# First attention: the causal mask moved from TensorE to VectorE in phases 1 to 7, and filling tiles moved

## The chip, the cores and the metric

One core of a Trainium2 chip runs the whole kernel. The metric is the device time of one execution in microseconds (us). The kernel before took 2174.97 us (median of three runs, 2171.95 to 2177.67).

## What is computed

Two transformer blocks over 512 tokens of width 1024. The change lies in the attention of the first block, which has 8 query heads of width 64 in two groups of four. Its selected branch and its window branch both reduce here to causal softmax attention over all 512 keys, because 16 selected blocks of 64 keys would be more than the 8 there are and the window is as long as the sequence:

```
def masked_softmax(logits, mask):
    logits = jnp.where(mask, logits, NEG)
    return jnp.where(mask, jax.nn.softmax(logits, axis=-1), 0.0)

# per query block of 128
pc  = masked_softmax(qb @ kc.T, cmp_end <= t)      # compressed keys, 31 of them
o_c = pc @ vc
ps  = masked_softmax(qb @ ks.T, kpos <= t);  o_s = ps @ vs
pw  = masked_softmax(qb @ kw.T, kpos <= t);  o_w = pw @ vw
o   = gates[0] * o_c + gates[1] * o_s + gates[2] * o_w
```

## The kernel before

Every matrix product is made of three fp32r matmuls (high by high, high by low, low by high). TensorE carries the whole kernel; ScalarE makes the high parts, VectorE and GpSimd the low ones.

The heads are taken in four pairs, one head of each group, both at once. A pair has two branches, so there are eight *phases* of four query blocks, 32 *steps* numbered here (phase, block). Even phases are the first branch, odd ones the second. `scores(j, i)` calls `head_scores` (L702 to L714): it waits until the exponentials of the step before have read PSUM banks 2 and 3 (`A["exps"]`), runs six matmuls (two heads in two halves of the array, three parts) over 128 to 512 keys, and then for each head one matmul of the identity with a 128x128 triangle of 0 and -1e30 (`causal_r`), which adds the mask to the diagonal block; the last one signals `A["scores"]`. VectorE's `head_peaks` (L1336 to L1339) waits for that and takes the negated row maximum of both heads; ScalarE's `head_exps` makes the two exponentials with their sums (L2003), `A["exps"]`; VectorE normalises (L1343, L1347). One phase later TensorE turns the probabilities (`turn`, L723), ScalarE copies the high part, VectorE's `head_low` subtracts for the low part (L1149, `A["lo"]`), and `values` multiplies (L731).

Once a pair, behind the last step of an odd phase, `cmp_scores` computes the logits of the next pair over the compressed keys into the same banks (L750 the mask, L756 24 matmuls of 32 columns). It waits for the exponentials; the next phase's first scores wait for VectorE's subtraction `s_cs["sub"]` (L1380). `cmp_turn` and `cmp_values`, which use a pair's compressed probabilities, stand in the first step of the even phase behind the pair (phases 2, 4, 6 and 8).

The waits of TensorE are covered by *filling tiles*: `fill(n)` runs n times three matmuls over 512 columns (L517 to L519) of the projections that are needed next (q of the next pair, the merge gates), 152 tiles in all. The order is written out by hand in `NSA_FILL`: one tuple a phase, one entry a step. The first number runs after the scores, the second at the step's end, the third (in steps (2,0), (4,0), (6,0), (8,0)) between `cmp_turn` and `cmp_values`. VectorE and ScalarE count the same numbers (`nsa_made`) to know which unit to evict after which step. VectorE's queue also carries the 31-tap convolution of the other branch of the block, two taps a step (L1209).

Each engine works its queue in order, and the queues meet only at semaphores.

Of the kernel before, what the change touches and what calls it, by code (L numbers as in the profile page):

```python
# [17 lines left out]
P = 128  # L18
# [148 lines left out]
EARLY_TAPS = 62  # L167
EARLY_IDLE = 8
LN_ADD = ((0, 1), (4, 0), (7, 3))
NSA_FILL = [((2, 2),) * 4] + [((2, 2),) * 4, ((2, 2, 2), (2, 1), (2, 2), (2, 1))] * 4  # L170


def nsa_made(j, i):
# [35 lines left out]
def build(nc, x_in, p_in, weights, vectors, last_gain, out):  # L209
# [4 lines left out]
    with ExitStack() as ctx:  # L214
# [145 lines left out]
        def stage_sems(stage, *names):  # L360
            return {n: sem(f"{stage}_{n}") for n in names}
# [6 lines left out]
        s_ln = stage_sems("ln", "sum", "mean", "cent", "sq", "acc", "var", "sd", "inv", "bc", "n", "act", "hi", "lo")  # L368
        s_mix = stage_sems("mix", "a", "b", "hi", "lo")
        att_names = ("scores", "peak", "exps", "inv", "probs", "turned", "hi", "lo", "pv", "ohi", "olo")  # L370
        A1 = stage_sems("nsa", *att_names, "q", "qhi")
        s_cs = stage_sems("cmp_att", "scores", "sub", "exp", "stat", "probs")
        A2 = stage_sems("fox", *att_names, "qk", "qkhi", "vturned", "vhi", "vlo", "crow")
        s_fg = stage_sems("forget", "dve", "act")
# [139 lines left out]
        def _(pe):  # L514
# [186 lines left out]

            def head_scores(A, s, qi, terms):  # L702

                if s:
                    pe.wait_ge(A["exps"], 2 * s)
                n = (qi + 1) * P
                qs = slice(qi * P, n)
                for t, (a, b) in enumerate(terms):
                    for hd in range(2):
                        rows = slice(hd * HD, (hd + 1) * HD)  # L710
                        pe.matmul(ps[:, 2 + hd, 0:n], a[rows, qs], b[rows, 0:n], start=t == 0, stop=False)  # L711
                for hd in range(2):
                    mm = pe.matmul(ps[:, 2 + hd, qs], ident_r[:], causal_r[:], start=False, stop=True)  # L713
                mm.then_inc(A["scores"], 1)  # L714

            def head_turn(A, y, kb, probs):
# [21 lines left out]
            def fill(n):  # L738

                for at in range(made[0], made[0] + n):  # L740
                    part(u0 + at // DC, at % DC, at % DC + 1)
                made[0] += n
# [55 lines left out]
            for j in range(9):  # L798
                b = j - 1
                for i in range(QB):  # L800
                    pieces = NSA_FILL[j][i]
                    if j < 8:
                        if j == 0 and i == 0:
                            cmp_scores(0)
                            fill(pieces[0])
                        scores(j, i)
                    if j or i:
                        fill(pieces[0])
                    else:
                        gates_turn()  # L810
                    if j == 8 and i == 0:
                        pe.wait_ge(s_ln["sum"], 3)
                        pe.wait_ge(A1["exps"], 64)
                        pe.matmul(ps[:, 2, :], mean_ch[:], ln_sum[:], start=True, stop=True).then_inc(s_ln["mean"], 1)
                    if b >= 0:
                        if i:
                            values(b, i - 1)
                        elif b:
                            values(b - 1, QB - 1)
                            if b % 2:  # L820
                                cmp_turn(b // 2)
                                fill(pieces[2])
                                cmp_values(b // 2)
                        turn(b, i)
                    if j % 2 and i == QB - 1 and j < 7:
                        cmp_scores(j // 2 + 1)
                    fill(pieces[1])
            fill(4)
            values(7, QB - 1)
# [309 lines left out]
        def _(dve):  # L1139
# [195 lines left out]

            def head_peaks(A, s, qi, st):  # L1336

                dve.wait_ge(A["scores"], s + 1)
                dve.tensor_reduce(st[:, 0, :, qi:qi + 1], ps[:, 2:4, 0:(qi + 1) * P], AX.X, ALU.max, negate=True).then_inc(A["peak"], 1)  # L1339

            def head_normalise(A, s, qi, st, probs, gate=None):
# [1161 lines left out]
```

## Time and profile before

| | us |
|---|---|
| median of three runs | 2174.97 |
| the profiled execution | 2177.95 |
| its span, first to last instruction | 2176.2 |
| TensorE busy | 2145.6 |
| VectorE, ScalarE, GpSimd busy | 1005.7, 873.2, 933.2 |

Busy times overlap, and matmuls are pipelined, so TensorE's busy time is no measure of its peak. The first attention lies between about 123 and 345 us of the span. Mean granted clock of TensorE: 0.995 of full speed.

### The profile page before, as it was taken

How to read it: one execution, taken by the hardware profiler on the slowest of the kernel's cores; microseconds unless marked ns; L12 is line 12 of the kernel's file. 1: busy time of each engine (PE TensorE's matmuls, PEld its weight loads, DVE VectorE, ACT ScalarE, POOL GpSimd, SP SyncE). 2: the span in 40 equal slices, each digit the busy share in tenths (PEclk: the TensorE clock that was granted, in tenths of full speed). 3: DMA queues.
4: the chain of work that ended last, by engine and by line, in shares of the span. 5: the costliest groups of instructions: out<-in, count | busy, mean ns of one | idle time of the engine just before them, and what ended most of it. 6: DMA issues, size and time to landing. Idle time of an engine off the chain costs nothing.

```text
span 2176.2 us, 25317 instructions
## 1 busy us (share of the span) xinstructions
PE 2145.6 (99%) x10198; PEld 1758.0 (81%) x10198; DVE 1005.7 (46%) x1630; ACT 873.2 (40%) x1366; POOL 933.2 (43%) x424
## 2 busy tenths in 40 slices
PE   9999999999999999999999999999999999999998
PEld 7877778888888887777778888888888888888886
DVE  5887775355525235566535422314643354222134
ACT  5444345344424254555434422324532244233234
POOL 5731224444444455322235444444554454444446
PEclk9999999999999999999999999999999999999999
DMA  4421113233333232211122223332223323233322
GB/s 160 151 82 40 49 40 95 89 107 97 97 97 97 97 112 83 68 49 59 49 68 88 97 97 97 97 97 84 91 90 98 95 86 97 97 97 97 97 82 84
DMA packets 53829, 193.27 MB, mean 89 GB/s; under 512 B 6096, under 2 KB 6224, under 8 KB 53712
## 3 DMA queue, kind: packets, MB, share of 16 engines
q1 hardware_dynamic: 52992, 189.81, 27.6%
q10 hardware_dynamic: 720, 1.84, 0.3%
q8 instruction: 81, 1.33, 0.2%
q14 instruction: 36, 0.29, 0.0%
HBM read 189.53 MB, written 2.10 MB: 88 GB/s over the span
## 4 chain that ended last, share of the span: by engine, by line
PE 91%; DVE 4%; ACT 3%; issue 1%; DMA 0%; POOL 0%; DVEq 0%; ACTq 0%; POOLq 0%
PE ps L517 27%; PE ps L519 27%; PE ps L518 27%; PE ps L731 1%; PE ps L980 1%; PE ps L711 1%; ACT w_hi L1854 1%; PE ps L723 1%; PE ps L998 1%; PE ps L613 1%; ACT fprob L1993 1%; PE ps L1005 1%; DVE xg_lo L1169 1%; PE ps L713 0%; PE ps L1007 0%
## 5 line engine op out<-in xcount | busy, mean ns | idle before, releaser
L470 POOL TENSOR_TENSOR w_lo<-w_raw,w_hi 128x1024 fp32r<-128x1024 f32 x352 | 851.8, 2421 | 1203.8 <-ACT w_hi L1854 1203.7
L517 PE MATMUL ps<-xg_hi,w_hi 128*128 128x512 f32 x1688 | 672.6, 398 | 4.5 <-POOL w_lo L484 2.4
L519 PE MATMUL ps<-xg_hi,w_lo 128*128 128x512 f32 x1688 | 660.0, 391 | 0.0
L518 PE MATMUL ps<-xg_lo,w_hi 128*128 128x512 f32 x1688 | 659.5, 391 | 0.0
L1854 ACT ACTIVATE w_hi<-w_raw 128x1024 fp32r<-128x1024 f32 x352 | 372.2, 1057 | 626.8 <-PE ps L519 623.9
L517 PEld LDWEIGHTS ps<-xg_hi,w_hi 128*128 128x128 f32 x1688 | 318.2, 189 | 68.1 <-issue 2.6
L519 PEld LDWEIGHTS ps<-xg_hi,w_lo 128*128 128x128 f32 x1688 | 317.9, 188 | 67.4
L518 PEld LDWEIGHTS ps<-xg_lo,w_hi 128*128 128x128 f32 x1688 | 318.5, 189 | 59.7
L517 PE MATMUL ps<-h_hi,w_hi 128*128 128x512 f32 x688 | 267.6, 389 | 0.0
L518 PE MATMUL ps<-h_lo,w_hi 128*128 128x512 f32 x688 | 267.6, 389 | 0.0
L519 PE MATMUL ps<-h_hi,w_lo 128*128 128x512 f32 x688 | 267.6, 389 | 0.0
L1143 DVE TENSOR_TENSOR ps<-ps,inv_rms 128x512 f32<-128x512 f32 x164 | 113.6, 695 | 194.2 <-PE ps L519 181.1
L517 PEld LDWEIGHTS ps<-h_hi,w_hi 128*128 128x128 f32 x688 | 129.1, 188 | 27.0
L519 PEld LDWEIGHTS ps<-h_hi,w_lo 128*128 128x128 f32 x688 | 129.1, 188 | 26.7
L518 PEld LDWEIGHTS ps<-h_lo,w_hi 128*128 128x128 f32 x688 | 129.1, 188 | 26.7
L1499 DVE TENSOR_TENSOR mixed<-mixed,ps 128x512 f32<-128x512 f32 x48 | 33.0, 687 | 200.0 <-PE ps L519 200.0
L1169 DVE SCALAR_TENSOR_TENSOR xg_lo<-resid,vec,xg_hi 128x512 fp32r<-128x512 f32 x72 | 87.2, 1215 | 12.5 <-ACT xg_hi L1880 10.3
L1209 DVE SCALAR_TENSOR_TENSOR ps<-glu,vec,ps 128x512 f32<-128x512 f32 x116 | 87.1, 751 | 1.8
L1843 ACT ACTIVATE h_hi<-ps 128x512 fp32r<-128x512 f32 x86 | 51.5, 599 | 89.7 <-DVE ps L1760 48.8
L1880 ACT ACTIVATE xg_hi<-resid,vec 128x512 fp32r<-128x512 f32 x72 | 51.7, 718 | 63.4 <-DVE resid L1499 40.2
L479 POOL TENSOR_TENSOR sq_sum<-sq_sum,sq 128x512 f32<-128x512 f32 x42 | 66.4, 1581 | 24.6 <-ACT sq L1877 22.3
L1760 DVE TENSOR_TENSOR ps<-tile_b,ps 128x512 f32<-128x512 f32 x64 | 44.5, 696 | 57.7 <-ACT tile_b L2301 57.7
(344 smaller groups left out, 2459.3 us busy)
## 6 DMA issues: line engine op xcount, KB each, us to landing
w_raw<-in_weights SPq DMA_DIRECT2D x352, 512.0 KB, 3.5
out_x<-mixed SPq DMA_DIRECT2D x8, 256.0 KB, 2.1
resid<-in_x SPq DMA_DIRECT2D x3, 512.0 KB, 7.2
p_raw<-in_p ACTq DMA_DIRECT2D x3, 512.0 KB, 3.7
resid<-in_x SPq DMA_DIRECT2D x2, 256.0 KB, 3.6
last_gain<-in_last_gain SPq DMA_DIRECT2D x1, 512.0 KB, 4.5
w_raw<-in_weights SPq DMA_DIRECT2D x1, 256.0 KB, 3.7
w_raw<-in_weights ACTq DMA_DIRECT2D x1, 256.0 KB, 4.0
```

The lines of the kernel that those rows point to most:

```text
L470: pool.tensor_tensor(w_lo[:, slot, :], w_raw[:, u % RAW, :], w_hi[:, slot, :].bitcast(F32), ALU.subtract).then_inc(w_ready, 1)
L479: pool.tensor_tensor(sq_sum[:], sq_sum[:], sq[:, m % 2:m % 2 + 1, :], ALU.add).then_inc(summed, 1)
L517: pe.matmul(o, w, x, start=start, stop=False)
L518: pe.matmul(o, w, xl, start=False, stop=False)
L519: return pe.matmul(o, wl, x, start=False, stop=stop)
L1143: dve.tensor_tensor(out, ps[:, BANK[u]:BANK[u] + 1, :], R[:], ALU.mult).then_inc(done, 1)
L1169: dve.scalar_tensor_tensor(xg_lo[:, m:m + 1, :], X[:, m:m + 1, :], g, xg_hi[:, m:m + 1, :].bitcast(F32), ALU.mult, ALU.subtract).then_inc( ...
L1209: ins = dve.scalar_tensor_tensor(acc if k < CONV_TAPS - 1 else conv_acc[:, ct, :], src, w, acc, ALU.mult, ALU.add)
L1760: dve.tensor_tensor(t, T2[:, m % 2:m % 2 + 1, :], t, ALU.mult).then_inc(s_mlp["s"], 1)
L1843: act.activation(out, x, ACT.Copy, scale=scale).then_inc(done, 1)
L1854: act.activation(w_hi[:, u % RING, :], w_raw[:, u % RAW, :], ACT.Copy).then_inc(w_hi_ready, 1)
L1880: act.activation(xg_hi[:, m:m + 1, :], X[:, m:m + 1, :], ACT.Copy, scale=g).then_inc(prep_hi, 1)
```

## The change

From step (1,0) on, TensorE leaves the two mask matmuls out, and the last of the six score matmuls signals. VectorE adds the triangle to the diagonal block of both heads in PSUM, in place, in one instruction of 128x256, and waits for its own add before it takes the maximum. In phase 0 the mask stays where it was.

`NSA_FILL` changes in phases 1 to 8. Odd phases: step 2 has one tile fewer at its end; step 3 has two tiles between the last turn and `cmp_scores` and one behind it, where there were two behind (in phase 7, without compressed scores, the same numbers). Even phases: step 0 has one tile fewer at its end, step 3 one more. So one tile more stands ahead of the scores of steps (3,0), (5,0), (7,0), the fifth of their pair's eight. The sums per phase stay 16.

```diff
-NSA_FILL = [((2, 2),) * 4] + [((2, 2),) * 4, ((2, 2, 2), (2, 1), (2, 2), (2, 1))] * 4
+NSA_FILL = [((2, 2),) * 4] + [((2, 2), (2, 2), (2, 1), (2, 1, 2)), ((2, 1, 2), (2, 1), (2, 2), (2, 2))] * 4
...
-        A1 = stage_sems("nsa", *att_names, "q", "qhi")
+        A1 = stage_sems("nsa", *att_names, "masked", "q", "qhi")
...
-                        pe.matmul(ps[:, 2 + hd, 0:n], a[rows, qs], b[rows, 0:n], start=t == 0, stop=False)
-                for hd in range(2):
-                    mm = pe.matmul(ps[:, 2 + hd, qs], ident_r[:], causal_r[:], start=False, stop=True)
+                        mm = pe.matmul(ps[:, 2 + hd, 0:n], a[rows, qs], b[rows, 0:n], start=t == 0,
+                                       stop=s >= QB and t == len(terms) - 1)
+                if s < QB:
+                    for hd in range(2):
+                        mm = pe.matmul(ps[:, 2 + hd, qs], ident_r[:], causal_r[:], start=False, stop=True)
                 mm.then_inc(A["scores"], 1)
...
                     if j % 2 and i == QB - 1 and j < 7:
+                        fill(pieces[2])
                         cmp_scores(j // 2 + 1)
+                    elif j == 7 and i == QB - 1:
+                        fill(pieces[2])
                     fill(pieces[1])
...
+                diagonal = ps[:, 2:4, qi * P:(qi + 1) * P]
                 dve.wait_ge(A["scores"], s + 1)
+                if s >= QB:
+                    dve.tensor_tensor(diagonal, diagonal, causal_r[:].bitcast(F32).unsqueeze(1).to_broadcast([P, 2, P]),
+                                      ALU.add).then_inc(A["masked"], 1)
+                    dve.wait_ge(A["masked"], s - QB + 1)
                 dve.tensor_reduce(st[:, 0, :, qi:qi + 1], ps[:, 2:4, 0:(qi + 1) * P], AX.X, ALU.max, negate=True).then_inc(A["peak"], 1)
```

## Rows read from the trace of the kernel before

**Rows 1.** The page: busy time by engine; the chain that ended last.
```profile
PE 2145.6 (99%) x10198; PEld 1758.0 (81%) x10198; DVE 1005.7 (46%) x1630; ACT 873.2 (40%) x1366; POOL 933.2 (43%) x424
...
PE 91%; DVE 4%; ACT 3%; issue 1%; DMA 0%; POOL 0%; DVEq 0%; ACTq 0%; POOLq 0%
```

**Rows 2.** Groups by line, 120 to 345 us: count, busy us, mean ns, idle before.
```profile
L713 PE MATMUL ps<-causal_r,ident_r 128*128 128x128 f32 x64 | 14.4, 307 | 0.0
```

**Rows 3.** Busy time by stretch, PE PEld DVE ACT POOL; then clock, DMA share, GB/s.
```profile
189.70:213.70 24.00, 23.48 (x151) 18.68 (x150) 20.49 (x38) 10.28 (x26) 4.79 (x2) 1.00 0.16 53
```

**Rows 4.** Timeline of TensorE in step (3,0): start us, us, engine, line.
```profile
189.69 0.33 PE L711 MATMUL ps<-kk_hi,q_hi 64*128 64x128 f32 x2
...
190.17 0.44 PE L713 MATMUL ps<-causal_r,ident_r 128*128 128x128 f32 x2
190.44 0.45 PE L517 MATMUL ps<-xg_hi,w_hi 128*128 128x512 f32 x1
190.73 0.40 PE L518 MATMUL ps<-xg_lo,w_hi 128*128 128x512 f32 x1
```

**Rows 5.** Timeline of TensorE behind the compressed scores of (3,3).
```profile
212.12 0.50 PE L517 MATMUL ps<-xg_hi,w_hi 128*128 128x512 f32 x1
212.45 0.39 PE L518 MATMUL ps<-xg_lo,w_hi 128*128 128x512 f32 x1
```

**Rows 6.** Groups of VectorE by line and shape, 120 to 345 us.
```profile
L1149 DVE TENSOR_TENSOR pt_lo<-ps,pt_hi 128x256 fp32r<-128x256 f32 x8 | 3.4, 419 | 2.0 <-ACT pt_hi L1843 2.0
...
L1143 DVE TENSOR_TENSOR ps<-ps,inv_rms 128x512 f32<-128x512 f32 x3 | 2.1, 688 | 0.0
```

**Rows 7.** Timeline of VectorE, steps (2,1) to (2,3); in brackets its idle time.
```profile
176.46 0.69 DVE L1339 TENSOR_REDUCE stat<-ps 128x2 f32<-128x512 f32 x1
...
185.43 0.69 DVE L1149 TENSOR_TENSOR pt_lo<-ps,pt_hi 128x512 fp32r<-128x512 f32 x1 [0.36 <-ACT pt_hi L1843]
...
186.73 1.23 DVE L1339 TENSOR_REDUCE stat<-ps 128x2 f32<-128x1024 f32 x1
...
189.47 0.17 DVE L1343 RECIPROCAL stat<-stat 128x2 f32<-128x2 f32 x1 [0.85 <-ACT prob_s L2003]
189.67 1.00 DVE L1347 TENSOR_SCALAR prob_s<-prob_s,stat,gates 128x512 f32<-128x512 f32 x2
```

**Rows 8.** Timeline of TensorE: first scores of step (2,1).
```profile
174.90 0.39 PE L711 MATMUL ps<-kk_hi,q_hi 64*128 64x256 f32 x2
```

**Rows 9.** Timeline: phase 2's first turned tile, subtraction and values.
```profile
195.71 1.23 DVE L1149 TENSOR_TENSOR pt_lo<-ps,pt_hi 128x1024 fp32r<-128x1024 f32 x1 [0.23 <-ACT pt_hi L1843]
...
197.15 0.40 PE L731 MATMUL ps<-pt_hi,vv_hi 128*128 128x512 f32 x1
```

**Rows 10.** Timeline, TensorE and VectorE, scores (3,1) to scores (4,0).
```profile
194.88 0.38 PE L711 MATMUL ps<-kk_hi,q_hi 64*128 64x256 f32 x2
...
197.50 0.69 DVE L1339 TENSOR_REDUCE stat<-ps 128x2 f32<-128x512 f32 x1
...
207.48 1.23 DVE L1339 TENSOR_REDUCE stat<-ps 128x2 f32<-128x1024 f32 x1 [0.56 <-PE ps L713]
...
210.33 0.41 PE L750 MATMUL ps<-cmp_mask_r,ident_r 128*128 128x128 f32 x2 [0.52 <-ACT prob_w L2003]
...
212.84 0.42 DVE L1380 TENSOR_TENSOR prob_c<-ps,c_stat 128x248 f32<-128x248 f32 x1
...
213.71 0.33 PE L711 MATMUL ps<-kk_hi,q_hi 64*128 64x128 f32 x2
```

**Rows 11.** Waits of TensorE, 120 to 345 us: total, times, longest.
```profile
PE ps L750 <- ACT prob_w L2003: 1.6, 3, 0.5
```

**Rows 12.** Busy time by stretch, columns as in rows 3.
```profile
163.90:167.30 3.40, 3.40 (x13) 2.26 (x12) 0.84 (x3) 0.41 (x1) 0.00 (x0) 0.51 0.02 5
...
259.70:266.50 6.80, 6.80 (x25) 5.16 (x24) 2.83 (x8) 2.16 (x6) 0.99 (x1) 0.51 0.00 0
```

**Rows 13.** Waits of VectorE, 120 to 345 us.
```profile
DVE pt_lo L1149 <- ACT pt_hi L1843: 28.7, 25, 3.1
```

## Prediction

> **What bounds the kernel now.** I read the page first: TensorE is busy 99% of the span and carries 91% of the chain that ended last [rows 1]. So a matmul taken away is worth its slot, unless another engine is late at that place. The change touches only the first attention, about 127 to 307 us. Its stage has two more things to see. In the list of groups, the causal-mask matmuls are 64 [rows 2], two a step. In the table by stretch, phase 3 (189.7 to 213.7) keeps VectorE busy 20.49 of 24.0 us [rows 3], convolution taps included, and what is left is mostly waiting inside its own loop (for exponentials, for turned probabilities). So VectorE is close to being the second bound here. I call a step (phase, query block), both from 0; mask changes are in phases 1 to 7, 28 steps.
>
> The loop of a step: scores (TensorE) -> maximum (VectorE) -> two exponentials (ScalarE) -> next scores, since banks 2 and 3 are used once at a time. Tiles that fill stand between.
>
> **Part 1, TensorE loses 56 mask matmuls.** Before: mask pair 190.17, first filling matmul 190.44, second 190.73 [rows 4]. With a mask the second filling matmul starts 0.29 after the first; where no mask stands between (after the compressed scores), 212.12 to 212.45, 0.33 [rows 5]. So a step saves 190.44 - 190.17 = 0.27 to 0.28 less 0.04 for the switch of the array that moves to the filling matmul: 0.24. 28 x 0.24 = **-6.7 us**. The signal of the scores also comes some 0.3 earlier, worth something only where VectorE is idle.
>
> The Trainium skill speaks against this size: "TensorE: Matmul & The Clock Gate", section "Back-to-back issue gap", gives about 81 ns for each 128-column matmul in a stream with its weight load. By it the pair costs 0.16 us and the change would bring, as an estimate, 28 x 0.16 = 4.5 us, 2.2 us less than my term. The rows show 0.27 for the pair, so the trace doesn't agree, and I keep it.
>
> **Part 2, VectorE gets 28 adds of 128x256 in PSUM, each with a wait for itself.** The trace has no such add. Nearest: the subtraction 128x256 out of PSUM, 0.419; the 128x512 product PSUM to PSUM, 0.688 [rows 6]. The maximum may start only when the add has landed: a reciprocal of 0.17 started at 189.47 and its successor, which waits for it, at 189.67, so 0.03 to 0.04 on top [rows 7]. I take 0.46, by the subtraction, which has the same width; ends 0.34 (half of the 512-wide product, no wait) and 0.72 (all of it, with the wait). In all 28 x 0.46 = 12.9 us of VectorE. Whether it costs depends on where VectorE leads the chain. Three places:
>
> *The fifth step of a pair, (2,3) to (3,0), three times.* From the maximum of (2,1) at 176.46 to that of (2,3) at 186.73 VectorE has only 0.36 us of waiting [rows 7], so it works 10.27. After: two more adds, 10.27 + 0.92 - 0.3 = 10.9. The maximum of (2,1) came 1.56 after its scores (174.90 [rows 8]); now + 0.46 for its own add and + 0.69 because one filling tile fewer stands at the end of (2,0) and the scores come that much nearer to VectorE's long subtraction: 2.71. From the maximum of (2,3) to the end of its exponentials, which released the reciprocal at 189.47, are 2.74 [rows 7]. Sum 16.35. TensorE walks from scores (2,1) to scores (3,0) in 189.69 - 174.90 = 14.79 [rows 4, 8], less 3 x 0.24, plus 0.69 for the tile moved ahead: 14.76. So it waits some 1.5 us where it waited next to nothing: 3 x 1.5 = **+4.5** (ends 0.5, if VectorE drops more waiting than I see, and 1.9). The moved tile pays for only 0.69 of it.
>
> *Values after the second scores of an odd phase, four times.* The subtraction of phase 2's first turned tile runs 195.71 to 196.94 and the matmuls that read it start at 197.15 [rows 9]: slack 0.21. Its chain goes back through ScalarE's queue (exponentials of (3,0), w_hi, q_hi, o_hi, then the turned tile) to the maximum of (3,0), which comes 0.46 later, while TensorE arrives two masks (0.48) earlier: 0.46 + 0.48 - 0.21 = 0.73. Not every phase has q_hi and o_hi in that queue, so I take 0.6: 4 x 0.6 = **+2.4** (ends 0 and 4.1).
>
> *Compressed scores, three times.* Now TensorE waits 0.52 for the exponentials of (3,3) [rows 10]; 1.6 us in all three [rows 11]. TensorE's way from scores (3,1) 194.88 to 210.33 is 15.45, 14.8 without the wait; after, less 0.72 for masks, plus 0.69 (one tile fewer at the end of (3,2), two before the compressed scores), plus the 0.6 just found: 15.4. VectorE: maximum (3,1) 2.62 after its scores, now about 3.6; from it to the maximum of (3,3) 207.48 - 197.50 = 9.98, less 0.56 of waiting that goes, plus 0.92: 10.34; 2.74 to the end: 16.7. Wait 1.2 or so instead of 0.65: the moved filling thus doesn't remove this wait. Behind them only one filling tile stands (two before) ahead of scores (4,0), which need VectorE's subtraction; it ended 213.26 and the scores came at 213.71 [rows 10], slack 0.45, now 0.45 - 0.69: a new wait of 0.24, or 0.45 when VectorE comes late to them. Together 0.55 + 0.35 = +0.9 each (ends 0 and 1.9): **+2.7**.
>
> *Moves themselves.* 152 filling tiles before and after, no DMA or copy added. Each new block of filling after a turn costs one start, 0.1: +0.3. The weights keep up: GpSimd, which makes their low parts, is busy 4.79 of 24.0 us [rows 3].
>
> Sum: -6.7 + 4.5 + 2.4 + 2.7 + 0.3 = **+3.2 us**.
>
> **The clock.** In two stretches right behind compressed scores the granted clock is 0.51, TensorE at 1.2 GHz: 3.4 us at 163.9 and 6.8 us at 259.7; behind the ones at 210.33, the last of phase 3, it stayed at 1.00, 2.4 GHz [rows 3, 12]. Both falls come just after TensorE had waited some 0.5 us [rows 11] and then run the narrow matmuls of the compressed scores. Cost 0.49 x 3.4 + 0.49 x 6.8 = 5.0 us in this execution. It took 2177.95 (span 2176.2 and 1.75 around); the median of the runs, 2174.97, is 2.98 lower, so a typical run seems to lose some 2 us here. The idle ahead of these places gets longer, not shorter; the full-width tile that is now put directly before them speaks for fewer falls. I take half a fall more, 0.5 x 2.5 = +1.2.
>
> From the execution's own time: 2177.95 + 3.2 + 1.2 - 2.98 = 2179.4 (the same from the median: 2174.97 + 4.4).
>
> **Rivals.**
> A, faster: VectorE hides the adds in its waits (28.7 us before subtractions of turned tiles alone [rows 13]), the compressed scores find their exponentials ready and the clock holds. Then 2174.97 - 6.7 - 2.0 - 2.1 + 0.3 = 2164.5. For it: that sum is twice 12.9. Against it: most of them lie just behind the compressed scores, where slack was several us anyway; the tight stretches have 0.36. Chance 0.12.
> B, slower: the longer idle before the compressed scores makes the clock fall every time. It decides once TensorE idles there for longer than now (0.65 with the switch) in all three. Three falls of 2.5 are 7.5 against 2 typical: 2174.97 + 3.2 + 5.5 = 2183.7; one more fall at the new waits of the fifth step, 2186. Against: the wait at 210.33 was as long as the others and the clock held [rows 3, 10]. Chance 0.30.
> C, break-even: the three waits come at half (9.6 to 4.8), since one wait absorbs the next one's lag: 2174.97 - 6.7 + 4.8 + 0.3 = 2173.4. Chance 0.20.
> My forecast, +3 to +6.5: 0.38 (its own range 2178 to 2182).
>
> **Numbers.** What can be told from no change is 0.3%, 6.5 us: faster is below 2168.4, slower above 2181.5. Slower: most of B (0.25) and the upper quarter of the forecast (0.10): 0.35. Faster: most of A: 0.10. Same 0.55. The range leaves out half of A and the end of B: 2167 to 2187. The fifth step and the compressed scores take 2 adds each, the values one: 16 adds on the chain, so an add of 0.34 takes 1.9 us off and one of 0.72 puts 4.2 on.
>
> **What would show it.** Right: the profile after shows VectorE adds near 0.43; mask matmuls 8; scores (3,0), (5,0), (7,0) preceded by TensorE idle of over 1 us ended by ScalarE's exponentials; new waits of the values matmuls on VectorE's subtraction; the wait before compressed scores above 0.5. Wrong: waits of TensorE in 142 to 307 under 3 us in all (then A), or a clock below 1.00 for over 15 us of the stage (then B). If the pair of mask matmuls was really 0.16, the pitch from last scores to second filling matmul shrinks less than 0.24.

## The result

| | device us, median | lowest to highest | runs |
|---|---|---|---|
| before | 2174.40 | 2171.95 to 2177.67 | 6 |
| after | 2186.64 | 2185.51 to 2190.18 | 6 |

The ratio is 1.0059 with a 95% interval of 1.0049 to 1.0069: 12.2 us slower, clear of what such a measurement can tell. The forecast was 2179.4; the result lies at the upper end of its range, beside rival B's second figure (2186). The profiled execution took 2186.16 us, span 2184.4.

Later runs of the kernel before bring it to 95 (median 2174.77). Two executions that were slow throughout (one of before, 3825.87 us; one of mixed_tap, 2368.89) are left out. Each run comes with its mean granted clock, so its span (the time less 1.75 us) can be split: span x (1 - mean clock) is lost to TensorE's slower level, and the rest of the span is work and waits. I use this split throughout. It takes half of every moment at the lower level as lost work; one run's clock is read to 0.001, 2.2 us, so only means say something (with their standard errors). The loss is that of the whole span: in every profile some 3 us of it lie in the last 15 us, and single falls come elsewhere too, with or without the change. Only differences between kernels speak of the change.

| kernel | runs | mean us | lost to the clock | the rest |
|---|---|---|---|---|
| before | 95 | 2174.5 | 5.9 +- 0.3 | 2166.9 +- 0.2 |
| after | 6 | 2187.1 | 12.4 +- 0.5 | 2172.9 +- 0.7 |

Of +12.6 us in the means, 6.0 are work and waits and 6.5 are the clock.

**The profile after.** The page: busy time by engine, and the chain that ended last. TensorE's share of the chain fell from 91% [rows 1] to 86%; VectorE's and ScalarE's doubled or nearly so.
```profile
PE 2143.4 (98%) x10142; PEld 1753.2 (80%) x10142; DVE 1017.6 (47%) x1658; ACT 872.4 (40%) x1366; POOL 933.2 (43%) x424
...
PE 86%; DVE 8%; ACT 5%; issue 1%; DMA 0%; POOL 0%; DVEq 0%; ACTq 0%; POOLq 0%
```
Groups by line in the stage (count, busy us, mean ns, idle before): 8 mask matmuls are left of 64 [rows 2], and the addition costs what its neighbour of the same width costs [rows 6], 426 ns.
```profile
L716 PE MATMUL ps<-causal_r,ident_r 128*128 128x128 f32 x8 | 1.8, 301 | 0.0
...
L1348 DVE TENSOR_TENSOR ps<-ps,causal_r 128x256 f32<-128x256 f32 x28 | 11.9, 426 | 2.6 <-PE ps L712 2.6
```
Waits of TensorE in 120 to 345 us (total, times, longest), to be held against rows 11. L712 are scores, L753 compressed scores, L734 values, L817 the mean of the LayerNorm. They sum to 12.6 us, 9.8 of them not the LayerNorm's; before had 1.6 at the compressed scores and 0.9 elsewhere (a wait of 0.2 ahead of the first compressed scores, which every kernel has, is left out).
```profile
PE ps L712 <- ACT prob_s L2015: 3.9, 6, 1.0
PE ps L753 <- ACT prob_w L2015: 3.0, 3, 1.3
PE ps L817 <- DVE ln_sum L1427: 2.8, 1, 2.8
PE ps L734 <- DVE pt_lo L1155: 2.3, 5, 0.9
PE ps L712 <- DVE prob_c L1392: 0.6, 3, 0.2
```
TensorE's timeline at the places of rows 4, 9, 10: scores (3,0), values of phase 2's first tile, compressed scores, scores (4,0); in brackets how long it had idled. The first wait began at about 190.87 and is the forecast's fifth step; 0.86 is the values' wait; 0.89 answers to 0.52 [rows 10].
```profile
191.90 0.33 PE L712 MATMUL ps<-kk_hi,q_hi 64*128 64x128 f32 x2 [1.03 <-ACT prob_s L2015]
...
192.71 0.39 PE L518 MATMUL ps<-xg_lo,w_hi 128*128 128x512 f32 x1
...
199.95 0.47 PE L734 MATMUL ps<-pt_hi,vv_hi 128*128 128x512 f32 x1 [0.86 <-DVE pt_lo L1155]
...
213.80 0.41 PE L753 MATMUL ps<-cmp_mask_r,ident_r 128*128 128x128 f32 x2 [0.89 <-ACT prob_w L2015]
...
216.77 0.33 PE L712 MATMUL ps<-kk_hi,q_hi 64*128 64x128 f32 x2 [0.23 <-DVE prob_c L1392]
```
From these scores to the second filling matmul are 192.71 - 191.90 = 0.81, before 190.73 - 189.69 = 1.04 [rows 4]: the mask's slot was 0.23.

VectorE's timeline ahead of that first wait (rows 7 are the same stretch before). The subtraction, one convolution tap (L1215), the addition, the maximum (L1351), then ScalarE's exponentials, which release the reciprocal at 191.88 and TensorE's scores at 191.90. The addition is late by the tap and by everything ahead of it.
```profile
187.41 0.69 DVE L1155 TENSOR_TENSOR pt_lo<-ps,pt_hi 128x512 fp32r<-128x512 f32 x1 [0.36 <-ACT pt_hi L1855]
188.02 0.75 DVE L1215 SCALAR_TENSOR_TENSOR ps<-glu,vec,ps 128x512 f32<-128x512 f32 x1
188.67 0.43 DVE L1348 TENSOR_TENSOR ps<-ps,causal_r 128x256 f32<-128x256 f32 x1
189.13 1.23 DVE L1351 TENSOR_REDUCE stat<-ps 128x2 f32<-128x1024 f32 x1
...
191.88 0.17 DVE L1355 RECIPROCAL stat<-stat 128x2 f32<-128x2 f32 x1 [0.85 <-ACT prob_s L2015]
```
Something I hadn't foreseen, at the end of the stage: VectorE's last LayerNorm addition started 0.19 us behind a subtraction on GpSimd and took 2.70 us, and TensorE waited for it.
```profile
313.38 2.34 POOL L470 TENSOR_TENSOR w_lo<-w_raw,w_hi 128x1024 fp32r<-128x1024 f32 x1 [3.78 <-ACT w_hi L1866]
...
313.57 2.70 DVE L1427 TENSOR_TENSOR ln_sum<-ln_sum,conv_acc 128x512 f32<-128x512 f32 x1
...
316.32 1.51 PE L817 MATMUL ps<-ln_sum,mean_ch 128*128 128x512 f32 x2 [2.84 <-DVE ln_sum L1427]
```
Table by stretch (columns of rows 3), behind the first and the third compressed scores and behind that last wait. At 0.76 to 0.85 a part of the stretch is at the 1.2 GHz level (each of these three falls cost 1.7 us in all, the first running on past its stretch); behind the second compressed scores it held 2.4 GHz throughout.
```profile
163.81:168.00 4.19, 4.01 (x36) 3.33 (x37) 3.12 (x8) 0.54 (x2) 0.00 (x0) 0.85 0.07 24
...
213.80:218.00 4.20, 3.97 (x38) 3.24 (x39) 3.44 (x9) 0.54 (x2) 0.00 (x0) 1.00 0.06 22
...
262.81:270.00 7.19, 7.02 (x49) 5.80 (x50) 5.58 (x14) 2.29 (x7) 0.57 (x1) 0.76 0.01 2
...
316.30:324.00 7.70, 7.68 (x33) 5.70 (x34) 1.25 (x2) 1.12 (x2) 0.00 (x0) 0.78 0.19 68
```
The two profiled executions happen to lose the same in the stage, 5.1 us each by a table in steps of 2.5 us, so between these two the clock explains nothing. The 6.5 us show only in the means over all runs.

### The profile page after: what moved, and what is told of

It reads as the page before. It is cut to its first block, busy times and chain, and to the rows that moved or that the text cites. A ratio compares the mean times of both kernels' runs of the same rounds, so it can differ in the third digit from the quotient of the medians.

```text
span 2184.4 us, 25233 instructions
## 1 busy us (share of the span) xinstructions
PE 2143.4 (98%) x10142; PEld 1753.2 (80%) x10142; DVE 1017.6 (47%) x1658; ACT 872.4 (40%) x1366; POOL 933.2 (43%) x424
## 4 chain that ended last, share of the span: by engine, by line
PE 86%; DVE 8%; ACT 5%; issue 1%; DMA 0%; POOL 0%; DVEq 0%; ACTq 0%; POOLq 0%
PE ps L517 27%; PE ps L519 26%; PE ps L518 26%; DVE stat L1351 1%; ACT w_hi L1866 1%; PE ps L986 1%; DVE ps L1215 1%; DVE pt_lo L1155 1%; PE ps L1004 1%; PE ps L613 1%; ACT prob_w L2015 1%; ACT fprob L2005 1%; PE ps L1011 1%; ACT pt_hi L1855 1%; DVE xg_lo L1175 0%
## 5 line engine op out<-in xcount | busy, mean ns | idle before, releaser
L1175 DVE SCALAR_TENSOR_TENSOR xg_lo<-resid,vec,xg_hi 128x512 fp32r<-128x512 f32 x72 | 86.4, 1204 | 12.2 <-ACT xg_hi L1892 10.0
L1215 DVE SCALAR_TENSOR_TENSOR ps<-glu,vec,ps 128x512 f32<-128x512 f32 x116 | 87.1, 751 | 1.9
L1164 DVE TENSOR_TENSOR sq_sum<-sq_sum,ps 128x512 f32<-128x512 f32 x57 | 39.1, 687 | 69.4 <-ACT ps L1883 69.0
```

What stands on the lines that cost most here:

```text
L1164: dve.tensor_tensor(sq_sum[:], sq_sum[:], ps[:, NB:NB + 1, :], ALU.add).then_inc(summed, 2 if m == DC - 2 and in_two_parts(n) else 1)
L1175: dve.scalar_tensor_tensor(xg_lo[:, m:m + 1, :], X[:, m:m + 1, :], g, xg_hi[:, m:m + 1, :].bitcast(F32), ALU.mult, ALU.subtract).then_inc( ...
L1215: ins = dve.scalar_tensor_tensor(acc if k < CONV_TAPS - 1 else conv_acc[:, ct, :], src, w, acc, ALU.mult, ALU.add)
```

## The experiments

Sixteen kernels. Theory 1: VectorE's additions make it late at a few places, TensorE idles there, and its clock falls behind the idling. A ratio is taken against executions of the kernel before that ran beside the kernel in question.

| kernel | us, median | ratio, 95% interval | lost to the clock | the rest |
|---|---|---|---|---|
| adds_old_fill | 2185.22 | 1.0049 [1.0037, 1.0062] | 10.0 +- 1.5 | 2173.6 +- 1.5 |
| fill_only | 2171.93 | 0.9990 [0.9981, 0.9999] | 6.3 +- 0.7 | 2164.6 +- 0.3 |
| masks_gone | 2168.92 | 0.9976 [0.9965, 0.9986] | 5.9 +- 0.9 | 2161.5 +- 0.7 |
| ln_early | 2185.34 | 1.0046 [1.0033, 1.0058] | 11.8 +- 1.5 | 2171.0 +- 0.8 |
| both | 2188.08 | 1.0057 [1.0045, 1.0069] | 11.4 +- 1.1 | 2174.0 +- 0.5 |
| ln_late | 2175.12 | 1.0003 [0.9994, 1.0011] | 6.7 +- 0.9 | 2166.9 +- 0.5 |
| ln_later | 2179.70 | 1.0026 [1.0016, 1.0036] | 9.0 +- 1.0 | 2168.9 +- 0.6 |
| taps_spread | 2184.52 | 1.0045 [1.0033, 1.0057] | 10.5 +- 1.3 | 2171.4 +- 0.6 |
| taps_spread_pe | 2178.45 | 1.0016 [1.0007, 1.0025] | 6.1 +- 0.3 | 2170.7 +- 0.3 |
| stuffed | 2182.39 | 1.0043 [1.0030, 1.0056] | 7.9 +- 1.5 | 2173.6 +- 0.9 |
| tap_behind | 2178.62 | 1.0024 [1.0014, 1.0034] | 10.3 +- 0.7 | 2167.0 +- 0.6 |
| adds_last | 2174.26 | 1.0000 [0.9991, 1.0009] | 8.3 +- 0.9 | 2165.0 +- 0.6 |
| mixed | 2177.36 | 1.0011 [1.0003, 1.0020] | 7.3 +- 0.5 | 2167.8 +- 0.3 |
| mixed_tap | 2173.34 | 0.9992 [0.9983, 1.0001] | 7.5 +- 0.7 | 2164.0 +- 0.2 |
| stuffed_values | 2177.88 | 1.0016 [1.0007, 1.0025] | 9.1 +- 0.9 | 2167.4 +- 0.5 |
| tap_behind_pe | 2171.48 | 0.9991 [0.9982, 0.9999] | 7.1 +- 0.7 | 2163.8 +- 0.5 |

### Which part costs: four kernels

**adds_old_fill**: the mask moved, the filling as before.
```diff
-NSA_FILL = [((2, 2),) * 4] + [((2, 2), (2, 2), (2, 1), (2, 1, 2)), ((2, 1, 2), (2, 1), (2, 2), (2, 2))] * 4
+NSA_FILL = [((2, 2),) * 4] + [((2, 2),) * 4, ((2, 2, 2), (2, 1), (2, 2), (2, 1))] * 4
```


> The adds and the missing mask matmuls of the change, with the filling order of before. Theory 1 (VectorE's queue is late, and the adds lie on the chain at the fifth step, at the values and at the compressed scores): waits of TensorE for exponentials before compressed scores above 1.5 us each, 1.2 to 1.8 us before scores (3,0), (5,0), (7,0); time 2183 to 2190, as slow as the change. Rival (the moved filling tiles make the loss, since one tile fewer stands before scores (2k,0) and at the end of (2k,0)): near 2172.

**fill_only**: the new filling, the masks on TensorE, no additions (the first line of the change's diff and the three fill(pieces[2]) lines alone).

> The new filling order alone, masks on TensorE. Theory 1: the waits before the compressed scores (0.5 us each) go, others stay, 2171 to 2176; clock falls behind the compressed scores fewer than before. Rival (the moved tiles make the loss): 2180 or more.

**masks_gone**: neither masks on TensorE nor additions, from phase 1 on.
```diff
-                if s >= QB:
-                    dve.tensor_tensor(diagonal, diagonal, causal_r...
-                    dve.wait_ge(A["masked"], s - QB + 1)
```


> The change without VectorE's adds: the causal mask of phases 1 to 7 is left out altogether, so the output differs. Theory 1: 28 x 0.24 us less of TensorE and no new waits beyond 0.5 us: 2166 to 2170. If the mask pairs were worth only 0.16 us each, 2170 to 2173. Rival (the time is lost by the shorter score groups or by the clock, not by the adds): 2178 or more.

**ln_early**: the last LayerNorm addition a step earlier.
```diff
-LN_ADD = ((0, 1), (4, 0), (7, 3))
+LN_ADD = ((0, 1), (4, 0), (7, 2))
```


> The change, with the last addition of the LayerNorm sum one step earlier in VectorE's queue (after step (7,2) instead of (7,3)). In the changed kernel that addition took 2.70 us (0.68 before) while GpSimd's subtraction ran, TensorE waited 2.84 us for it and its clock fell to 0.50 behind. Theory 2 (this is the loss that the forecast lacks, 5 us): wait of the mean matmul for ln_sum gone, no fall at 317 us, 2180 to 2183. Rival (the wait is that of the lagging exponentials of (7,3), and would only be named otherwise): 2185 to 2188.

The additions are the loss, whatever the filling: masks_gone, without them, is as fast as expected. With the old filling TensorE's waits at the six places are longest (1.14 to 1.72 us, one of the three at the compressed scores below the 1.5 expected), and in this profile the clock falls behind each of the six: the table by stretch of adds_old_fill behind its compressed scores (first, third and fifth line) and behind the first scores of phases 3, 5 and 7 (second, fourth and sixth).
```profile
163.50:169.50 6.00, 6.00 (x38) 4.63 (x37) 3.45 (x9) 0.95 (x4) 0.00 (x0) 0.72 0.01 3
190.00:197.00 7.00, 5.83 (x30) 5.11 (x31) 5.22 (x14) 4.21 (x13) 0.98 (x1) 0.76 0.19 69
214.50:220.50 6.00, 6.00 (x32) 4.62 (x32) 4.15 (x11) 2.16 (x6) 0.00 (x0) 0.72 0.02 4
241.00:248.00 7.00, 5.82 (x30) 5.15 (x31) 5.70 (x14) 4.19 (x12) 0.98 (x1) 0.76 0.17 67
265.00:272.00 7.00, 7.00 (x49) 5.59 (x48) 4.79 (x12) 1.88 (x6) 0.00 (x0) 0.76 0.01 2
291.00:300.00 9.00, 7.55 (x39) 6.04 (x39) 7.33 (x16) 4.98 (x12) 2.04 (x1) 0.81 0.16 58
```
Its waits (as above), then those of fill_only, where the ones of rows 11 are gone:
```profile
PE ps L712 <- ACT prob_s L2012: 5.3, 5, 1.7
PE ps L753 <- ACT prob_w L2012: 4.3, 3, 1.6
```
```profile
PE ps L711 <- ACT prob_s L2006: 0.7, 2, 0.4
PE ps L731 <- DVE pt_lo L1152: 0.3, 1, 0.3
```
But idling isn't needed for a fall. fill_only came in at its expected time, yet its clock loss, 6.3, is no lower than before's 5.9, though fewer falls were expected. Its table by stretch, where TensorE's compressed scores ran from 211.00 to 212.7 with no idle ahead of them:
```profile
210.00:212.50 2.50, 2.50 (x30) 2.21 (x30) 2.22 (x5) 0.47 (x3) 0.00 (x0) 1.00 0.41 162
...
215.00:217.50 2.50, 2.50 (x8) 1.92 (x7) 2.24 (x6) 1.75 (x5) 0.33 (x1) 0.50 0.00 0
```
masks_gone has such a fall behind its first compressed scores. So some falls come with the narrow matmuls of the compressed scores or what stands around them, and what the additions bring are falls more.

In the column "the rest" the change falls into three steps: the filling brings 2166.9 to 2164.6 (-2.3), taking the masks off 2164.6 to 2161.5 (-3.1), the additions 2161.5 to 2172.9 (+11.4), and their clock +6.5 (5.9 to 12.4). ln_early took the 2.8 us wait away and brought 1.9 of "the rest" (standard error of the difference 1.1); its addition took 1.12 us. The clock loss stayed, and at 2185.34 it missed the 2180 to 2183 expected: the LayerNorm is not the main part of the miss.

### The additions alone, and TensorE's idling filled

**both**: the kernel before, masks and filling as they were, plus the 28 additions (the first attention's VectorE lines of the diff alone).

> The kernel before, with its causal-mask matmuls and its filling kept, plus VectorE's 28 additions: the mask is added twice, which leaves the probabilities of masked keys at zero. It prices the additions alone. Theory 1 (the additions stretch the chain scores, maximum, exponentials; TensorE waits at the three places and its clock falls there more often): TensorE's waits as in the run with additions and the old filling (about 1.2 to 1.7 us at every compressed scores and at every first step of an even phase), the clock loss of the stage again near 10 us instead of 5, and the masks' 6.7 us on TensorE paid in part only, since at the steps with a wait they fill it: 2188 to 2193. Rival (the removal of the masks is itself what makes the clock fall, since TensorE is less busy): clock loss as before (5 us), 2183 or less.

2188.08, the highest of all. "The rest" rose by 7.1 and the clock loss by 5.5. The rival, that only a TensorE without masks has its clock fall, is out: here it has all of them. Beside adds_old_fill: 56 mask matmuls taken off, under the additions, bring 2.9 us in the median and 0.4 +- 1.6 in "the rest", since TensorE waits anyway.

**stuffed**: 24 matmuls more, where the changed kernel idled.
```diff
+            def again():
+                ...
+                three(o, wh, xh, wl, xl, k == 0, False)
+                pe.matmul(o, wh, xh, start=False, stop=k == 0)
...
                         fill(pieces[2])
+                        again()
                         cmp_scores(j // 2 + 1)
...
                     fill(pieces[1])
+                    if i == QB - 1 and j in (2, 4, 6):
+                        again()
```


> The changed kernel with 24 matmuls of 512 columns more on TensorE (four of them, 0.92 us, ahead of the compressed scores of phases 1, 3 and 5 and ahead of the first scores of phases 3, 5 and 7); they add one filling product again, so the output changes. They stand where TensorE waited 0.83 to 1.26 us in the changed kernel, so that it works instead of waiting. Theory 1 (TensorE's clock falls behind those waits): 5.5 us of work are added and 5.0 us or more of waits go, the sum of both stays within 1 us, and the clock falls of the stage become fewer: from a loss of 12 us (mean over the runs) to 7 or less, so that the kernel with more work is faster, 2179 to 2183. Rival (the falls have nothing to do with these waits): the same loss, 2186 to 2189; second rival (the work isn't hidden): 2190 or more.

Its waits: those ahead of scores fell from 3.9 to 0.9, of compressed scores from 3.0 to 0.3; the other two stayed.
```profile
PE ps L827 <- DVE ln_sum L1440: 2.8, 1, 2.8
PE ps L734 <- DVE pt_lo L1168: 2.2, 5, 0.9
PE ps L712 <- ACT prob_s L2028: 0.9, 3, 0.4
...
PE ps L763 <- ACT prob_w L2028: 0.3, 1, 0.3
```
By stretch behind three of the six places (ahead of the third it still idled 0.32) and behind the LayerNorm's wait, which both kernels keep; behind the other three the clock was 1.00 as in the first two lines:
```profile
163.00:168.00 5.00, 4.83 (x44) 3.95 (x45) 4.28 (x10) 1.11 (x6) 0.00 (x0) 1.00 0.04 15
189.00:195.00 6.00, 5.91 (x41) 4.62 (x39) 4.85 (x12) 3.21 (x11) 0.78 (x1) 1.00 0.16 60
...
260.00:268.00 8.00, 7.55 (x52) 6.34 (x53) 5.68 (x14) 2.58 (x10) 1.46 (x1) 0.79 0.04 13
...
313.80:321.50 7.70, 7.69 (x33) 5.80 (x34) 1.24 (x2) 1.16 (x2) 0.00 (x0) 0.78 0.22 68
```
The kernel with 5.5 us more work is 4.3 us faster, in the predicted interval: "the rest" is up by 0.7 and the clock loss down by 4.5 (standard error 1.6), to 7.9 where 7 or less was expected. This is the experiment that shows the clock following the idling.

All eighteen kernels say the same less sharply. A straight line through their mean clock losses against TensorE's waits in the stage by their profiles is 5.9 + 0.48 x waits (all in us; standard error of the slope 0.08, correlation 0.85), with kernels up to 1.9 off it. So about half a microsecond of clock goes with each microsecond of waits, and the changed kernel's 10.1 us more of waits would give 4.9 of its 6.5. The waits are those of one profile each. By the profiles, nearly all falls of the stage lie behind compressed scores, with or without idling there; only adds_old_fill (three, behind the first scores of phases 3, 5 and 7) and taps_spread (one, behind a wait of 1.9) have others, the one behind a long LayerNorm wait apart.

### The LayerNorm addition beside GpSimd

**ln_late** and **ln_later**: the kernel before with one, then two copies ahead of that addition.
```diff
+                    if (j, i) == LN_ADD[2]:
+                        for n in (0, 1):
+                            dve.tensor_copy(T[:, n, :], ps[:, NB, :])
                     if (j, i) in LN_ADD:
```


> The kernel before with one more VectorE copy of 512 columns (about 0.6 us) ahead of the third LayerNorm addition, so that the addition starts beside GpSimd's subtraction, as in the changed kernel, and nothing else of the change. Theory (the addition is stretched by GpSimd's work, not by anything of the masks): the addition goes from 0.68 to 2.3 to 2.8 us, TensorE waits 2.3 to 3 us ahead of the mean, and its clock falls behind that wait: 2176.5 to 2179. Rival (an effect of the changed kernel's memory or queues): the addition stays at 0.7 us, TensorE waits below 0.8 us, and the time stays within 1 us of before.

> The kernel before with two more VectorE copies of 512 columns ahead of the third LayerNorm addition. With one of them the addition still began 0.09 us ahead of GpSimd's subtraction and took 0.68 us; with two it begins about 0.5 us behind its start, as in the changed kernel (0.19 us behind). Theory (an addition of three SBUF tiles on VectorE that starts beside GpSimd's subtraction is held until that ends): 2.0 to 2.8 us, TensorE waits 2.5 to 3 us ahead of the mean, 2177 to 2180. Rival (the 2.70 us came from something else in the changed kernel): 0.68 us, TensorE waits 1.1 us, 2175 to 2176.

With one copy the expected did not happen, because the addition was still ahead of GpSimd by 0.09 us: it took 0.68, and GpSimd's subtraction, 2.34 elsewhere, took 2.82 (ln_late's timeline):
```profile
305.14 0.68 DVE L1415 TENSOR_TENSOR ln_sum<-ln_sum,conv_acc 128x512 f32<-128x512 f32 x1
...
305.23 2.82 POOL L470 TENSOR_TENSOR w_lo<-w_raw,w_hi 128x1024 fp32r<-128x1024 f32 x1 [4.85 <-ACT w_hi L1856]
```
With two it came behind (ln_later's):
```profile
308.47 2.34 POOL L470 TENSOR_TENSOR w_lo<-w_raw,w_hi 128x1024 fp32r<-128x1024 f32 x1 [4.84 <-ACT w_hi L1857]
...
308.98 2.38 DVE L1415 TENSOR_TENSOR ln_sum<-ln_sum,conv_acc 128x512 f32<-128x512 f32 x1
```
GpSimd ends at 308.47 + 2.34 = 310.81, the addition at 311.36, 0.55 later. In the changed kernel it is 315.72 and 316.27, again 0.55. So the second to start does its work when the first is through. TensorE waited 2.76 us and the kernel took 4.9 us more than before, in the expected interval: 2.0 in "the rest", 3.1 (standard error 1.0) at the clock. ln_late, with one copy less and the addition ahead, took 0.4 us more than before. The difference, some 4.6 us, is nearly all the price of the order of two instructions.

### Where in a step: VectorE's taps

**taps_spread** and **taps_spread_pe**: the taps dealt out by a table, with the mask on VectorE and on TensorE.
```diff
+EVEN_TAPS = ((1, 4), (0, 0), (1, 0), (2, 0))
+TAPS = [((2, 0), (2, 0), (1, 0), (3, 0))] + [((2, 0),) * 4, EVEN_TAPS] * 3 + [((2, 0), (2, 0), (2, 0), (0, 0))]
...
-                    if tapped[0] < CT * CONV_TAPS:
-                        taps(1)
+                    if j < 8:
+                        taps(TAPS[j][i][0])
```


> The changed kernel with the 62 convolution taps of VectorE's queue dealt out otherwise in phases 0 to 7 (two a step in odd phases; in even phases five in the first step, four of them behind the low parts of the compressed probabilities, then none, one and two), and the third LayerNorm addition at (7,2). Each tap is about 0.7 us of VectorE, so this takes up to 1.4 us off VectorE's queue at the steps where TensorE waited, and puts it where VectorE had idle time. Theory 1 (the loss is VectorE's lateness at three places, and the clock falls that follow): the waits at the compressed scores, at the first steps of even phases and at the values fall below 0.3 us each, the clock loss of the stage goes from 12 us to below 6, and the 6.7 us of mask matmuls come out as a gain: 2163 to 2169. Rival (the clock falls come from TensorE's thinner stream of instructions without the masks, not from the waits): clock loss stays near 10 us, 2173 to 2180.

> The same deal of taps and the new filling with the causal mask left on TensorE (no additions on VectorE): the control for the run above. It shows what of that run's gain comes from the taps and what from moving the mask. Theory 1: before this deal TensorE's waits were 1 us at most with this filling, so there is little to win: 2168 to 2173, 3 to 7 us above the run with the mask on VectorE. Rival (the deal of taps is the gain): within 1.5 us of that run, or faster.

Both missed. The waits I aimed at shrank (ahead of scores 3.9 to 0.6, of compressed scores 3.0 to 1.7) but did not all fall below 0.3, and others came, for turned tiles. Waits of taps_spread:
```profile
PE ps L736 <- DVE pt_lo L1157: 9.3, 9, 1.9
```
The main reason, read from VectorE's trace and not tested by a run of its own, is that of the LayerNorm addition again. With two taps ahead of it, the normalisation (L1361) of the first and third step of every odd phase runs into GpSimd's subtraction and ends only behind it. Such a pair of instructions takes 0.60 us at 128 columns and 0.87 at 384 elsewhere; here, all four times, 2.43 to 2.45 and 2.94 to 2.95. First the mean of the eight at 128 columns (344 ns in fill_only), then one pair with GpSimd's instruction:
```profile
L1361 DVE TENSOR_SCALAR prob_w<-prob_w,stat,gates 128x128 f32<-128x128 f32 x8 | 9.8, 1259 | 0.1
```
```profile
196.33 2.40 POOL L472 TENSOR_TENSOR w_lo<-w_raw,w_hi 128x1024 fp32r<-128x1024 f32 x1 [6.39 <-ACT w_hi L1867]
196.63 2.45 DVE L1361 TENSOR_SCALAR prob_w<-prob_w,stat,gates 128x128 f32<-128x128 f32 x2
```
Over the eight steps that is 15.6 us more of VectorE. The control has the same eight, also 15.6 us, and is 6.5 us slower than fill_only without any addition. No other kernel here has one such step. So these two runs say little on dealing the taps: they show a collision that the deal brought about.

**tap_behind**: one tap moved, and only at the fourth query block, plus ln_early's edit.
```diff
                     if tapped[0] < CT * CONV_TAPS:
-                        taps(1)
+                        taps(2 if i == 3 and j < 7 else 1)
...
-                    if tapped[0] < CT * CONV_TAPS:
+                    if tapped[0] < CT * CONV_TAPS and not (i == 2 and j < 7):
                         taps(1)
```


> The changed kernel with the third LayerNorm addition at (7,2) (its own run: 2185.3) and, in phases 0 to 6, the convolution tap (0.75 us) that stood ahead of VectorE's addition at the fourth query block moved behind it and the maximum, where VectorE waits for ScalarE's exponentials. Theory 1 (what costs is the lateness of that addition at the six places): the addition starts up to 0.65 us earlier, the waits ahead of the compressed scores fall from 0.8 to 1.3 us to 0.2 to 0.6 us, those of the first scores of odd phases from 1.0 to 0.4 us, and the clock loss falls by 2 to 5 us: 2176 to 2181. Rival (the loss is spread over all 28 additions and TensorE's thinner stream): 2184 to 2186. A tap behind may also make the normalisation late where the exponentials are quick; then the turns wait, and the time stays.

**tap_behind_pe**: the same on fill_only.

> The new filling with the masks on TensorE (2171.9), the tap moved as in the run with the moved tap, and the third LayerNorm addition at (7,2). Here TensorE waits 0.5 us at most, so theory 1 expects nothing of the tap's move: 2171 to 2173, and the value of moving the mask is the difference to 2178.6, a loss of 6 to 7 us. Rival (the tap ahead of the maximum costs in every version): 2167 to 2170.

Both times are as expected. Seven taps moved by one place brought 6.7 us with the additions (against ln_early) and 0.5 without (against fill_only, which lacks ln_early's edit too). In the means it is 5.5: 4.0 +- 1.0 in "the rest", and 1.5 +- 1.6 at the clock, which shows no change there; 2 to 5 was expected. VectorE's timeline (compare the one above): the addition follows the subtraction at once, two taps run while ScalarE makes the exponentials, and TensorE's wait is 0.34 instead of 1.03.
```profile
184.28 0.69 DVE L1155 TENSOR_TENSOR pt_lo<-ps,pt_hi 128x512 fp32r<-128x512 f32 x1 [0.36 <-ACT pt_hi L1855]
184.89 0.42 DVE L1348 TENSOR_TENSOR ps<-ps,causal_r 128x256 f32<-128x256 f32 x1
185.34 1.23 DVE L1351 TENSOR_REDUCE stat<-ps 128x2 f32<-128x1024 f32 x1
186.49 1.54 DVE L1215 SCALAR_TENSOR_TENSOR ps<-glu,vec,ps 128x512 f32<-128x512 f32 x2
188.08 0.17 DVE L1355 RECIPROCAL stat<-stat 128x2 f32<-128x2 f32 x1
```

### Seven of the 28

**adds_last**: fill_only plus the additions of the fourth query block. **mixed**: ln_early without those seven. **mixed_tap**: tap_behind without them.
```diff
-                if s < QB:
+                if s < QB or qi == QB - 1:
                     for hd in range(2):
...
-                if s >= QB:
+                if s >= QB and qi < QB - 1:
                     dve.tensor_tensor(diagonal, diagonal, ...
```


> The kernel before with the new filling (2171.9) and the masks on TensorE, plus VectorE's addition at the fourth query block of phases 1 to 7 alone (7 of the 28; at these the mask is added twice). All 28 additions with the masks kept cost 13 us. Theory 1 (the additions cost where TensorE has no work behind the scores, that is at the end of each phase): these seven carry most of it, 2178 to 2182, with waits of 0.8 us or more at the compressed scores or first scores, and a clock loss of 9 us or more. Rival (each addition costs alike): 7/28 of 13 us, 2174 to 2176, clock loss 6 to 7.5 us.

> The changed kernel with the third LayerNorm addition at (7,2) (2185.3) and the causal mask of the fourth query block of every phase back on TensorE: 21 steps on VectorE instead of 28. Theory 1 (lateness at the end of each phase is what costs): 7 x 0.23 = 1.6 us of mask matmuls come back, the waits at the compressed scores and first scores fall from about 1.0 us by the addition's 0.46 and the mask's 0.23 to about 0.3 us, clock loss from 12 to 7 to 9: 2175 to 2179. Rival (each addition costs alike, 13/28 = 0.46 us each): 2185.3 - 7 x 0.46 + 1.6 = 2183.7.

> The same with the convolution tap moved behind the maximum of the fourth query block (2178.6 with all 28 additions). Theory 1: the tap's 0.65 us covers what was late there, so the waits at the six places are gone, and 21 x 0.23 = 4.8 us of TensorE's work is saved; what stays are the waits at the values of odd phases (0.86 us once, 0.36 us three times): 2169 to 2174, the first version with the mask on VectorE that is not slower than before. Rival (the clock loss of 10 us comes from TensorE's thinner stream, which this keeps in 21 of 28 steps): 2176 to 2179.

The same seven additions cost 2.3 us where they are the only ones (adds_last, the rival's size), and 8.0 us where the other 21 stand too (ln_early against mixed, 1.6 us of mask slots that came back not counted). adds_last thus missed what theory 1 expected, and mixed met it (2177.36, clock loss 7.3). So the places are right, but no addition has a price of its own: where these seven stand alone they go into VectorE's spare time, and behind the other 21 they come out in TensorE's. The two pairs differ in one thing more, which no run separates: adds_last keeps all the masks on TensorE, and their slots give VectorE time. mixed_tap, as expected, is the only kernel with the mask mostly on VectorE that is not slower than before; nor is it faster than fill_only.

**stuffed_values**: tap_behind with two matmuls more ahead of the values of each odd phase's second step.
```diff
                         if i:
+                            if i == 1 and j % 2:
+                                again()
                             values(b, i - 1)
```


> The kernel with the moved tap (2178.6) and two matmuls of 512 columns more (0.46 us) ahead of the values of the second step of phases 1, 3, 5 and 7, where TensorE waited 0.55, 0.86, 0.38 and 0.36 us; the output changes by the added products. Theory 1 (the clock falls behind these waits too): the work is hidden but for 0.2 us, the waits go, the clock loss falls from 10 us to 7 or less: 2175 to 2177. Rival (these waits are too short to matter): clock loss stays at 10, 2178.5 to 2180.

Inconclusive. The waits at values fell from 3.2 to 1.4 us and the time by 0.7; the clock loss of 9.1 +- 0.9 lies between the two expectations.

## Why the prediction was wrong

By its own steps, in means over runs:

- **The clock, forecast +1.2, measured +6.5.** This is the step that failed. I took "half a fall more" by splitting the difference between two arguments, though I had forecast 9.6 us of new waits in the same text and had two falls in front of me, each behind an idle of 0.5 us. The number of falls was not worked out from the waits. Their price wasn't too low: 2.5 was taken, and each fall in the profile after and in adds_old_fill cost 1.7, so 6.5 us are some four of these more, not half a one (both has longer ones, of 3.4 and 5.2). The argument that a full-width tile directly ahead of the compressed scores speaks for fewer falls isn't borne out: fill_only has that tile, no idle there, and a loss of 6.3. Rival B had the mechanism and mostly the place. But in the profile after, the clock fell behind the compressed scores twice of three times, not every time, and its figure of 2186 is right in part by luck: it had +3.2 of work and waits and some 8 of clock, where 6.0 and 6.5 were measured. My own sign for it, 15 us of the stage below 1.00, isn't in the profile after (some 10 us): one profile is too few to read a mean clock loss from.
- **The additions' waits, forecast +9.6, measured +9.5** in "the rest" (masks_gone to ln_early, standard error 1.1). The places hold, the sizes were taken too large, and the agreement is in part luck. In the profile after, TensorE's waits without the LayerNorm's rose by 7.3 us (2.5 to 9.8), and at the places forecast by some 6.6: 3 x 1.0 for the fifth step (I said 1.5); none, 0.86, 0.36 and 0.36 for the four values (0.6); 0.83, 0.89 and 1.26 for the compressed scores (1.2), and 0.17 to 0.23 behind them (0.24). One more of 0.36 came at the values of step (4,2), which I hadn't named. Against masks_gone (1.9) the waits rose by 7.9; what makes up the other 1.6 of "the rest", if it isn't noise, I can't say. The addition is 0.43 to 0.46, the value taken.
- **The masks, forecast -6.7, measured -3.1 +- 0.8** (fill_only to masks_gone). The slot is as read, 0.23. The Trainium skill ("TensorE: Matmul & The Clock Gate", "Back-to-back issue gap") would have given, as an estimate, 0.16; the trace does not agree. But a slot taken off TensorE is time only where nothing else is late: in the profile of masks_gone TensorE's waits rose by 0.9 us over fill_only's even without additions. The rest of the difference I can't place.
- **The moves, forecast +0.3 and no help to the wait ahead of the compressed scores, measured -2.3 +- 0.3.** On its own the moved filling takes that wait away altogether (rows 11 have no counterpart in fill_only), and most of the 2.3 are its 1.6. Masks and moves err by +3.6 and -2.6 and nearly cancel.
- **The LayerNorm addition, not in the sum, +1.9** in "the rest" and a fall of the clock behind it. Its parts were in view: the addition at 308.68 and GpSimd's subtraction at 309.37 in the trace of before, 0.7 us apart, in a stage that I forecast to shift. The Trainium skill states the rule ("SBUF — State Buffer", "SBUF: two separate sides"): VectorE and GpSimd share a port pair, and of a VectorE operation with two inputs in SBUF and a GpSimd operation that reads SBUF, whichever starts first holds it for its whole length. The trace agrees, both ways, at 0.55 us behind the end. The taps, with one input in PSUM, are not held: one that ran beside GpSimd's subtraction took 0.75 us as elsewhere (188.02 in the timeline after).

Check of the sum: 5.3 + 1.9 + 3.6 - 2.6 - 0.1 = 8.1, and 12.6 - 4.4 = 8.2.

What stays open: why tap_behind still loses 10.3 +- 0.7 us to the clock (ln_early 11.8 +- 1.5, the changed kernel 12.4 +- 0.5) with waits of 6.2 us instead of 9.8 and 12.6, and only one above 0.6; why the clock falls behind compressed scores ahead of which TensorE did not idle; and why one execution falls at a place where another holds.

## What to carry to other kernels

When an edit adds waits to the engine that sets the time, price them twice: the idling, and the clock falls that come with it, which here cost as much again; filling the idle with useless matmuls is a cheap test of the second. Work moved from a full engine to a nearly full one has no price per instruction: find the instruction that stands ahead of the moved one at the latest step (here one 0.75 us tap, worth 6.7 us over seven steps) before giving up or going on. And when a stage shifts, look for pairs of SBUF operations on VectorE and GpSimd that had just missed each other: this came up unforeseen twice here, at the LayerNorm and in taps_spread.

What beats both kernels, by 0.1% and with intervals that just exclude 1, are fill_only and tap_behind_pe, both with the masks on TensorE; and masks_gone, which leaves the mask out, shows what moving it could bring at most with this filling and these taps: 0.9976.

## What the runs showed of the hardware

- TensorE dropped to its 1.2 GHz level behind idle times of 0.5 to 2.8 us between dense matmuls, at some such places and not at others, and also behind compressed scores that it reached without idling (fill_only, masks_gone). More idling went with more loss: 24 matmuls put into gaps of 0.83 to 1.26 us gave 4.5 +- 1.6 us of clock loss back.
- A VectorE addition of three SBUF tiles, 0.68 us alone, took 1.12, 2.38 and 2.70 us when it started 1.83, 0.51 and 0.19 us behind the start of a GpSimd subtraction of 2.34 to 2.40 us, each time ending 0.55 us behind it; started 0.09 us ahead, it kept its 0.68 and GpSimd took 2.82.
- Two VectorE normalisations of 128x128 out of SBUF into SBUF, 0.60 us together, took 2.45 when the first started 0.30 us behind the start of such a subtraction (taps_spread), and ended 0.35 behind its end.
